# A hybrid decoder layer on one core: projection units in another order, with the recurrent chain and the head norms between them

## The reference, cut to what matters

```python
xn = rms_norm(h, g_mix)
u  = xn @ w_in                      # 1664 columns: lru 384, gate 384, q 384, k 128, v 128, qm 256
xc = causal_depthwise_conv(u_lru, conv_w, conv_b)              # width 4
y_lru = rg_lru(xc, ...) * gelu(u_gate)
#   r, i = sigmoid(xc @ w_a + b_a), sigmoid(xc @ w_x + b_x)    block-diagonal, 64 x 64 a head
#   a = exp(-8 r softplus(-lam)); state = a state + sqrt(1 - a^2) (i xc)   scan over the tokens
q, k, qm = rms_norm by head (64 features) of u_q, u_k, u_qm;  km likewise from the memory
y_swa = sliding_window_sink_attention(q, k, v, sinks)          # window 128, 6 heads on 2 key heads
y_mem = memory_cross_attention(qm, km, vm)                     # 4 heads, 256 memory tokens
y = concatenate([rms_norm(y_lru), rms_norm(y_swa), rms_norm(y_mem)])
h = h + y @ w_out
h = h + moe(rms_norm(h, g_ffn))     # 32 experts, the best 4 of each token
```

## Time and profile before

| | us |
|---|---|
| median of 3 runs | 2349.05 (2344.52 to 2350.45) |
| the profiled execution | 2345.39 |
| its span, first to last instruction | 2343.70 |
| PE busy | 2182.0 (93%) |
| DVE busy | 1399.1 (60%) |
| ACT busy | 1054.8 (45%) |
| POOL busy | 258.7 (11%) |
| stage of the projection units, 49.56 to 239.10 | 189.54 |
| from there to the first scores, 239.10 to 285.80 | 46.70 |
| attention, 285.80 to 418.36 | 132.56 |

### The profile page before, as it was taken

The page is one execution under the profiler, slowest core; times in us unless marked ns, Lnnn a source line. Parts: engine busy times, 40 slices in busy tenths (PEclk is TensorE's granted clock), DMA queues, the critical chain, the costliest instruction groups (busy, mean ns, idle before and its releaser), DMA issues.

```text
span 2343.7 us, 30087 instructions
## 1 busy us (share of the span) xinstructions
PE 2182.0 (93%) x9748; PEld 1615.6 (69%) x9749; DVE 1399.1 (60%) x1809; ACT 1054.8 (45%) x1256; POOL 258.7 (11%) x202
## 2 busy tenths in 40 slices
PE   6999678998599999999999999999999999999997
PEld 4454277544377887787687878787777887887885
DVE  4004566332777568757867666757877557567565
ACT  3023454111254446545645454545655445445444
POOL 1000300000111111101101010201111101002001
PEclk9999899898799999999999999999999999999998
DMA  7000200200587659958968595858988658558656
GB/s 248 0 1 0 99 1 1 90 27 28 188 317 285 197 183 341 339 194 300 350 226 286 206 304 184 295 191 304 342 323 291 201 190 287 173 193 302 187 183 223
DMA packets 201093, 473.43 MB, mean 202 GB/s; under 512 B 14695, under 2 KB 19879, under 8 KB 200992
## 3 DMA queue, kind: packets, MB, share of 16 engines
q1 hardware_dynamic: 183566, 433.75, 51.6%
q0 software_dynamic: 17424, 39.17, 7.1%
q10 hardware_dynamic: 66, 0.02, 0.0%
HBM read 464.53 MB, written 32.11 MB: 212 GB/s over the span
## 4 chain that ended last, share of the span: by engine, by line
PE 51%; DVE 9%; issue 7%; DMA 6%; ACT 6%; DVEq 1%; POOLq 1%; ACTq 0%; POOL 0%
PE ps L1049 13%; PE ps L1051 13%; PE ps L1050 13%; DMA out<-y,idx_cur 6%; PE ps L974 5%; DVE w_lo L1507 5%; ACT w_hi L716 3%; PE ps L1084 1%; PE ps L1106 1%; PE ps L1102 1%; DVE hm L1569 1%; PE ps L1043 1%; DVE onehot L1496 1%; ACT y L742 1%; PE ps L993 1%
## 5 line engine op out<-in xcount | busy, mean ns | idle before, releaser
L1507 DVE TENSOR_TENSOR w_lo<-ring,w_hi 128x2048 fp32r<-128x2048 f32 x349 | 796.5, 2288 | 337.5 <-ACT w_hi L716 337.4
L716 ACT ACTIVATE w_hi<-ring 128x2048 fp32r<-128x2048 f32 x346 | 655.5, 1914 | 381.8 <-PE ps L1051 355.1
L1049 PE MATMUL ps<-w_hi,xT_hi 128*128 128x512 f32 x1288 | 512.7, 398 | 26.7 <-ACT y L742 15.4
L1051 PE MATMUL ps<-w_hi,xT_lo 128*128 128x512 f32 x1288 | 503.2, 391 | 0.0
L1050 PE MATMUL ps<-w_lo,xT_hi 128*128 128x512 f32 x1288 | 502.9, 390 | 0.0
L1049 PEld LDWEIGHTS ps<-w_hi,xT_hi 128*128 128x128 f32 x1288 | 242.4, 188 | 87.9 <-issue 27.5
L1049 PE MATMUL ps<-w_hi,actT_hi 128*128 128x512 f32 x720 | 289.2, 402 | 0.0
L1051 PE MATMUL ps<-w_hi,actT_lo 128*128 128x512 f32 x720 | 281.9, 392 | 0.0
L1050 PE MATMUL ps<-w_lo,actT_hi 128*128 128x512 f32 x720 | 281.2, 391 | 0.0
L1050 PEld LDWEIGHTS ps<-w_lo,xT_hi 128*128 128x128 f32 x1288 | 242.3, 188 | 55.1 <-issue 4.5
L1051 PEld LDWEIGHTS ps<-w_hi,xT_lo 128*128 128x128 f32 x1288 | 242.1, 188 | 51.5
(11 more groups left out here) (264 smaller groups left out, 2001.0 us busy)
## 6 DMA issues: line engine op xcount, KB each, us to landing
ring<-in_w SPq DMA_DIRECT2D x390, 1024.0 KB, 5.2
xh<-in_x SPq DMA_DIRECT2D x2, 2048.0 KB, 17.6
work<-in_w_out SPq DMA_DIRECT2D x1, 4096.0 KB, 12.8
token_rows<-uT POOLq DMA_DIRECT2D x8, 512.0 KB, 2.9
out<-xh SPq DMA_DIRECT2D x8, 512.0 KB, 2.6
work<-in_w_in SPq DMA_DIRECT2D x2, 1536.0 KB, 19.3
uT<-in_w_mem_kv SPq DMA_DIRECT2D x1, 2048.0 KB, 17.7
ring<-in_w_in SPq DMA_DIRECT2D x2, 1024.0 KB, 15.3
```

The costliest lines, as they stand in the source:

```text
L716: act_e.activation(w_hi[s % SPLIT][:, :, :], slot(s), ACT.Copy).then_inc(hi_ready, counted(s, whole))
L1049: pe.matmul(acc, hi, whi, start=first, stop=False)
L1051: return pe.matmul(acc, lo, whi, start=False, stop=last)
L1507: return dve.tensor_tensor(lo, x, hi.bitcast(F32), ALU.subtract)
```

## The change

The units run in the order recurrent (6), K, Q, QM, gate, V. The first gate products stand behind eight units, the second and third behind three more each. The seven head sums stand between units, as do eight of the thirteen spreads; the last five follow the last unit. The scratch of the chain (`lru_s`), `rroot` and `headrow` lie in the input rows `xh`, so x is loaded a second time (`x_again`) before the residual. GELU and the product with it are taken out of the chain: ACT runs the three GELUs after the unit that follows the roots, DVE the three products (now L1324) after the head norms. POOL's squares wait for these. SP's first loads bring the recurrent weights, then `wB`, then the gate weights. `take_y` stands ahead of `softmax_in`. The zeroed key tiles and `kmz` change places.

The diff, cut to its core:

```diff
-        kz = [[ring[:, 7168 + g * S:7168 + (g + 1) * S], lru_tmp[:, 2 * g, :]] for g in range(2)]
-        kmz = lru_tmp[:, 1, :].rearrange("p (h m) -> p h m", h=NM)
+        kz = [[lru_tmp[:, 1, :], lru_tmp[:, 0, :]], [ring[:, 8192:9216], lru_tmp[:, 2, :]]]
+        kmz = ring[:, 7168:8192].rearrange("p (h m) -> p h m", h=NM)
+        lru_s = xh[:, 0:6, :]
...
-        units = [(h, c) for h in range(2) for c in range(6)]
-        units += [(h, c) for c in (K, V) for h in range(2)] + [(h, c) for c in (Q, Q + 1, Q + 2, QM, QM + 1) for h in range(2)]
+        units = [(h, LRU + c) for h in range(2) for c in range(LT)]
+        units += [(h, c) for c in (K, Q, Q + 1, Q + 2, QM, QM + 1, GATE, GATE + 1, GATE + 2, V) for h in range(2)]
...
+            sp.wait_ge(spread, len(norm_units))
+            sp.wait_ge(scanned, LT)
+            for i in range(2):
+                sp.dma_start(xh[:, 4 * i:4 * i + 4, :], xv[:, 4 * i:4 * i + 4, :]).then_inc(x_again[i], 16)
...
-            po.wait_ge(in_done, len(units))
+            po.wait_ge(scaled, 3)
+            po.wait_ge(sq_sum, 10)
             po.memset(rroot, 1.0).then_inc(pool_step, 1)
...
+            for i in range(8):
+                take_unit(i)
+            act_e.wait_ge(dve_const, 1)
+            for c in range(LT):
+                lru_gates(c)
+                for i in range(8 + 3 * c, 11 + 3 * c):
+                    take_unit(i)
+            norm_square(0)
+            norm_square(1)
+            for i in range(17, 22):
+                take_unit(i)
+                norm_square(i - 15)
+            take_unit(22)
...
+            for i in range(8):
+                unit(i)
+            for c in range(LT):
+                gate_products(c)
+                for i in range(8 + 3 * c, 11 + 3 * c):
+                    unit(i)
+            for n in range(len(normt)):
+                norm_sum(n)
+                unit(17 + n)
+            for u in range(4):
+                norm_spread(u)
+            unit(24)
+            for u in range(4, 8):
+                norm_spread(u)
+            unit(25)
+            for u in range(8, len(norm_units)):
+                norm_spread(u)
...
                 if c == 0:
-                    dve.wait_ge(in_done, 12)
-
+                    dve.wait_ge(scaled, 3)
+                    dve.wait_ge(sq_sum, 10)
+                else:
+                    dve.wait_ge(scanned, c)
+                    dve.wait_ge(gate_mm, 4 * c)
...
+                if j >= 2:
+                    take_y(j - 2)
                 if j + 2 < len(items):
                     softmax_in(j + 2)
-                if j >= 2:
-                    take_y(j - 2)
...
+                if i % 4 == 0:
+                    dve.wait_ge(x_again[i // 4], 16)
```

More of the change, by code:

```diff
@@ L206, in hymba_layer @@
         x_in = [sem(f"x_in{i}") for i in range(2)]
+        x_again = [sem(f"x_again{i}") for i in range(2)]
+        scanned = sem("scanned")
         wA_in = [sem(f"wA_in{i}") for i in range(2)]
@@ L851, in gate_products, with norm_sum @@
                     for h in range(2):
-                        pe.matmul(ps[:, 4 + 2 * g + h, :], gate_w[:, g, c, :], lru_tmp[:, 0, h * HALF:(h + 1) * HALF],
+                        pe.matmul(ps[:, 4 + 2 * g + h, :], gate_w[:, g, c, :], lru_s[:, 0, h * HALF:(h + 1) * HALF],
                                   start=True, stop=True).then_inc(gate_mm, 1)
-            for i in range(12):
-                unit(i)
-            for c in range(LT):
-                for i in range(12 + 5 * c, min(12 + 5 * c + 5, len(units))):
-                    unit(i)
-                gate_products(c)
-            pe.wait_ge(pool_const, NPOOLC)
-            pe.wait_ge(gate_act, 4 * LT)
-            for n, (t, w, g) in enumerate(normt):
+            def norm_sum(n):
+                t, w, g = normt[n]
+                if n == 0:
+                    pe.wait_ge(pool_const, NPOOLC)
+                    pe.wait_ge(gate_act, 4 * LT)
                 pe.wait_ge(nsq, n + 1)
@@ L877, in _ @@
                           rroot[:, h * HALF:(h + 1) * HALF], start=True, stop=True).then_inc(spread, 1)
+            for i in range(8):
+                unit(i)
+            for c in range(LT):
+                gate_products(c)
[12 more added lines that the diff above has]
+                norm_spread(u)
+            pe.wait_ge(in_out, len(units))
             pe.wait_ge(normed, len(norm_units))
@@ L1278, in _ @@
                 if n == 1:
-                    dve.wait_ge(kz_zero, 5)
+                    dve.wait_ge(kz_zero, 1)
                     for o in (0, 1):
@@ L1289, in _ @@
                                              op0=ALU.mult, op1=ALU.mult).then_inc(normed, 1)
+            for c in range(LT):
+                u = uT[:, LRU + c, :]
+                dve.wait_ge(scanned, c + 1)
+                dve.wait_ge(gelu_done, c + 1)
+                dve.tensor_tensor(u, u, uT[:, GATE + c, :], ALU.mult).then_inc(ylru, 1)
             scale = DH ** -0.5
```

72 lines of the change are left out of this document (32 added, 40 removed).

## The result

| | before | changed |
|---|---|---|
| median of 5 runs | 2349.05 us | 2334.84 us |
| lowest and highest | 2344.52, 2351.04 | 2326.86, 2335.18 |
| profiled execution, its span | 2345.39, 2343.7 | 2335.18, 2333.5 |
| ratio of the times, 95% interval | | 0.9936 [0.9926, 0.9947] |

The medians differ by 14.2 us, the two profiled executions by 10.2 us; 12.5 us were forecast. The profiled execution of before was one of its quicker runs and that of the changed kernel its slowest, which explains the gap between the two differences.

The account below looks back on a forecast made before the run. PE, never idle in the projection, then its idle pieces and the attention were taken to bound the kernel. 8.3 us ahead of the scores plus 4.2 us in the loop made 12.5 us: 2349.05 to 2336.5 us, range 2328 to 2345.

Parts of the forecast that it names:

- the price of the two-tile move: Attention loop: moving a two-tile output ahead of the next softmax step costs DVE 0.52 us, leaving 0.70 us gained per pair.
- the reordering: Stretch ahead of the attention: reordered units let the first scores start 8.6 us earlier, 8.3 us gained after a low-clock charge.
- the move: Attention loop: finished outputs moved ahead of the next softmax step save 0.70 us in each of six pairs, 4.2 us.
- The units and the chain: Projection: 24.0 us of PE work covers a 20.0 us recurrent chain between gate products, 4.0 us slack, twice, no stall.
- PE's end: Ahead of the attention: PE ends its last spread at 263.4 us, including 2.0 us of new idle time.
- SP's queue: Ahead of the scores: key copies move only after the output weights, so scores start at 277.2 us, PE idle 13.8 us.
- DVE after the scores: First scores to softmax: the scores' lead counts as gain, less 0.3 us for low clock on the first score bank.
- The rival with the copies free: Key copies do not queue behind the output weights: 22.9 us gained, 2326.2 us, or 2331.9 with POOL waits; chance 0.08.
- a cover of 9 us: Ahead of the scores: DVE's three gating products end at 267.9 us, 9 us before scores exist, so cost nothing.
- The chain that does not fit between the units: Projection: recurrent chain exceeds 24.0 us and PE idles twice; gain only 2 to 6 us, 2343 to 2347; chance 0.09.
- That the loop gets no shorter: Attention loop: exponentials and copies hold it, or the clock falls more often; gain 8.3 us, 2340.8 us; chance 0.13.
- that the attention loses its clock: Attention after 13.8 us of idle PE: mean clock 0.81 cancels the gain, 0.70 gives 2364.6 us; chance 0.05.

## Why the prediction was right, and where it was not

2336.5 us was forecast and 2334.84 measured, the gain 14.2 us for 12.5. The direction of both terms held, and their mechanism but for the price of the two-tile move. The sum, though, came out near only because two terms were mis-sized in opposite directions: the reordering 4.0 us instead of 8.3, the move 10.5 instead of 4.2 (in the order in which they were taken apart above). That part of the agreement is luck.

**The units and the chain: right.** Slack of 4.0 us between gate products was forecast, 3.6 us is there, and nothing stalls. The idle piece ahead of the first sum is 1.72 us for 2.0.

**PE's end: 2.0 us late** (265.4 for 263.4). The rate of uninterrupted groups was used for work that is now interleaved. A sum of four records with a unit behind it takes 8.88 us (178.55 to 187.42), not 1.72 + 6.9 = 8.6. There are seven such pieces, one with a sum of two records, and together they take 61.2 us (178.55 to 239.77) instead of 13 x 0.86 + 7 x 6.9 = 59.5: 1.7 us. The weight loads show the switch, though not what causes it: the loader is idle for 0.24 us ahead of a load inside a unit, and for more than three times as much at each change of group:

```profile
186.47 0.19 PEld L852 LDWEIGHTS ps<-work,ring 128*128 128x128 f32 x1 [0.24 <-issue]
187.42 0.11 PEld L875 LDWEIGHTS ps<-ring,headcol 128*14 128x14 f32 x2 [0.76 <-issue]
...
188.38 0.30 PEld L852 LDWEIGHTS ps<-work 128*128 128x128 f32 x2 [0.85 <-ACT uT L574]
```

**SP's queue: right.** The first scores start 18.4 us after the issue of the weights, forecast 18.0, and the kernel with the copies first confirms the cause. Their start (279.54 for 277.2) is late by the 1.9 us by which PE's last unit and with it the issue are late (261.12 for 259.2), which this queue hands on in full, and by 0.4 us.

**DVE after the scores: missed, 1.2 us.** I took the scores' lead as the gain. From the first scores to the first softmax step it takes 6.35 us, before 4.88; 0.3 us of this was charged. POOL beside DVE is 1.0 us of the 1.47 by the run with POOL late. The rival with the copies free named that cause, but only for the products. Behind a cover of 9 us these cost nothing, as forecast. It was not asked what else of DVE meets POOL's six operations: they end at 283.6, not at the 282.4 forecast, and the first COPYs fall among them. 8.3 - 1.9 - 0.4 - 1.2 = 4.8 us, the lead at the first softmax step; 4.0 to 4.3 us are left at the end of the kernel with the move undone.

**The move: the step that was furthest off.** The term was 6 x 0.70. A full pair saves 15.00 - 13.63 = 1.37 us. The 1.22 us that PE waited are 1.40 when gone: the copy stands 1.27 us behind the softmax step, before 2.67 (368.68 against 366.01). And the 0.52 us charged for the two-tile move are 0.03: without it DVE waits for score banks (0.12 and 0.17 us) in that very place, and its two scalings stand apart. From the start of the copy to that of the reduction behind the scalings it is 2.43 us with the move between and 2.40 without. The same two waits can be read in the kernel before. I had charged a move on a busy path without looking what the next instruction waits for. Five pairs at 1.37 are 6.9 us.

**The low clock in the loop: not in the sum.** In the last five pairs the kernel with the move undone takes 77.5 us (312.49 to 390.02), the changed one 68.2: 9.4 us, 2.5 more than 6.9. Pairs of 15.87 and 16.68 us, at clock 0.90, no longer occur; in all eleven kernels with the three-tile move ahead every pair from the third on is 13.59 to 13.65 us long. In a full pair of before PE stood still for 3.0 us (15.00 - 11.98, in pieces of 1.22, 1.12 and 0.68), with the two-tile moves alone for 3.2 (1.22 at L966 and 2.02 at L939), with the three-tile moves alone for 1.7 (0.99 at L956 and 0.69 at L939). Less standing still and a clock that stays up go together here; that the one makes the other was not tried apart. The price is in the first two pairs: 14.10 and 15.85 us at clocks 0.76 and 0.78, against 13.39 and 13.21 us with the move undone. That gives 3.4 us back, and 2.8 us more are won between the last pair and the first sums behind the attention. Why one pair is low and its like is not stays open. In the second pair of the changed kernel, and of the one with the move undone, PE stands for the same 2.54 us at the same place, at clock 1.00 before it; behind it the same 16 records run at 0.50 in the first and at 1.00 in the second:

```profile
303.87 3.68 PE L956 MATMUL ps<-vm,ring 128*128 128x64 f32 x16 [2.54 <-ACT ring L646]
```

```profile
303.17 2.00 PE L956 MATMUL ps<-vm,ring 128*128 128x64 f32 x16 [2.54 <-ACT ring L646]
```

The kernels with the copies on the other queue, and with products early, have first pairs of 13.5 and 13.9 us and second ones of 13.2.

**The rivals.** That the copies don't queue: refuted by their landing, 15.1 us against 4.0 in the kernel with the copies first. That kernel is what this rival described; it was priced at 22.9 us of gain, or 17.2 with the wait on POOL, and measured 27.8, some 6 us of which are the mis-sized move. The rule of the Trainium skill on the port shared by DVE and GpSimd (SBUF — State Buffer, section "SBUF: two separate sides") agrees with the trace, but I had counted two waits of 2.84 us where the three products show 5.19 - 3.49 = 1.7 us: the second product ran first, POOL waited for that, and only the third waited, for a square. The chain that does not fit between the units: refuted, PE stalls at no gate product. That the loop gets no shorter, and that the attention loses its clock: refuted. The argument against the last was read too kindly, for the clock of before was back at 1.00 by 289.8 but at 0.50 again from 298 to 300, and its first two pairs have 0.87 and 0.88. The loop is shorter, at a mean clock of 0.89 against the 0.91 of the earlier trace rows:

```profile
279.54:405.20 125.66, 103.95 (x669) 93.68 (x670) 86.42 (x177) 62.92 (x225) 3.96 (x2) 0.89 0.09 35
```

## What to carry to other kernels

A wait inside a loop is to be priced by the distance between two fixed rows of a period, with and without it: what is put in its place costs only what the next instruction would not have waited for anyway. In a queue that moves transfers in order, put the small urgent one first: exchanging two statements here brought 13.3 us, nearly as much as the whole change, while another queue brought the first scores only 2.3 us forward and slowed the large load. When an edit brings forward a group of POOL operations, list all of DVE's operations in the same stretch, not just those that hand over to it. And undo both halves of a change, each in the other's presence and without it: here their gains don't add up.

## What the hardware did that I had not expected

- DVE's COPY of 128x256 from SBUF to SBUF beside POOL: up to 2.00 us instead of 0.28, though some still took 0.28. Even operations of 128x4 and 128x6 stretch: L1360 took 0.82 us in the kernel with the copies first, 0.17 in the changed one; with POOL late a `DVE L1375` of the 128x6 size took 1.57 us while a square ran.
- PE's loader stands idle for 0.76 and 0.85 us at a switch between a unit and a sum, against 0.24 us within a unit.
- 1,024 KB of copies on ScalarE's queue beside 4,096 KB on SP's took 10.4 to 12.1 us, alone ahead of them 4.0 to 4.6 us; the large load grew from 13.9 to 20.3 us.
- The granted clock of the first two pairs was 0.76 and 0.78 although PE's gaps in them were of at most 2.96 us. These pairs hold fewer PE records (47 and 75) than the later ones (87), so they are no like for like; but second pairs with the same 75 records ran at 1.00 in the kernel with the copies on ScalarE's queue (13.21 us instead of 15.85).
